# A hybrid decoder step: the norm's gain moved from a GpSimd pass into the weight splits, and gates and scans of two blocks moved to other tiles

## The chip, the cores and the metric

One core of a Trainium2 chip runs the whole program. The metric is the device time of one execution in microseconds (us); lower is better. TensorE (PE) multiplies, VectorE (DVE), ScalarE (ACT) and GpSimd (POOL) do the rest, SyncE (SP) only issues transfers.

## The reference, cut to what matters

```python
def rmsnorm(x, g):
    y = xf * lax.rsqrt(jnp.mean(xf * xf, axis=-1, keepdims=True) + EPS)
    return (y * g.astype(jnp.float32)).astype(x.dtype)

xn = rmsnorm(x, norm_gain)                       # x: 16 meta + 2048 prompt tokens, 8x8 sample tokens, 1024 features
proj = jnp.einsum('btd,dp->btp', xn, w_in)       # 9 groups of 512 columns, and 8 gate columns
yc, conv_new = short_conv(gc * hc, conv_buf, conv_w)
y_conv = gb * yc * jax.nn.silu(zc)
h, state = mlstm_seq(q, k, v, ig, lf, state)     # chunks of 128 tokens, 4 heads of 128, state carried over
y_m = (rms(h) * mh_norm_gain * sigmoid(o)) * silu(zm)
out = jnp.einsum('btw,wd->btd', jnp.concatenate([y_conv, y_m], axis=-1), w_out)
return x + out, ...                              # then a final rmsnorm
```

Since `norm_gain` has one factor for each feature, that is for each row of `w_in`, the kernel multiplies it into the weights and not into the tokens.

## The kernel before, in words

Features lie on the 128 partitions, as KT = 8 groups k of 128 (`w[:, k, :]`). Every float32 operand of the projection is held as a sum of two float16 parts, high and low (`xTh`, `xTl` for the tokens, `Wh`, `Wl` for the weights, the latter scaled by WS = 64), and every product is three matmuls: high-high, low-high, high-low, at L824 to L826 (for the V tile L833 to L835).

The projection is done by **head group** g = 0 to 3 (128 columns of each of nine column groups). A head group has nine **weight tiles**, in the order K, V, Q, GC, HC, GB, ZC, O, ZM (t = 0 to 8), and four **blocks** b of 512 prompt tokens. `pe_block(g, b)` goes over the nine tiles, 24 matmuls of 512 columns each, into one of two PSUM banks in turn (`PB`); it waits on `p_free` until ACT or DVE has emptied the bank of two tiles earlier. In b = 0 each tile also gets a small product for the 80 meta and sample tokens into the bank `T0` ("mix"). Between the halves and at the ends of tiles TensorE does the recurrent part: transposes at L868, the arguments of the exponentials (A), scores (S), and at the ZC and O tiles four `chunk` steps (L887, L888, L893), each of which waits until DVE's `update` has brought the state `cn` forward for the chunk before.

Nothing is scheduled: each engine runs its own written list, in the order of tiles (`at_half`, `evacuate`, `at_end`), joined by semaphores. DVE and ACT wait for their own previous instruction before each one (class `Order`: `did` and `mark` count, `settle` waits; all of them are recorded at L163). So whatever stands first in an engine's list and waits, holds up all that is behind it.

**Weights.** A tile of `w_in` (128 x 1024 float32) is loaded into one of three buffers `wst`. Then three engines work on it in turn: POOL multiplies it by `gain` in place (`gain_w`, L610), ACT writes the high part `Wh` (`split_w`, one activation with scale 64), DVE writes the low part `Wl` = 64 w - Wh (`split_w`, one SCALAR_TENSOR_TENSOR). Only when DVE is done (`w_low`) may the buffer be loaded again. The nine tiles of head group 0 are split at the start and during block 0: t = 0 ahead of the blocks, 1 and 2 too, 3 at the V tile, and 4 to 8 at the half of the tiles Q, GC, HC, GB, ZC (`SPLIT_AT_HALF`). The nine tiles of head groups 1, 2, 3 are split during the last block (b = 3) of the head group before, tile t right after the same tile's own work ("weights blocks" below: (0, 3), (1, 3), (2, 3)); ACT issues the load of tile t + 2 behind its split of tile t.

**Tokens** are normalised in `x_square`, `x_power` (POOL), `x_high_part` (ACT) and `x_low_part` (DVE), and transposed by DMA, one 128-token unit after the other, those of block b + 1 during block b of head group 0.

**Gates.** In blocks 0 to 2 of head group 0, TensorE computes the gate logits of the next block at the end of the tile `GATES_AT[b]` (L849, L850, 16 matmuls into the bank `T1`), ACT and DVE take them from there; DVE runs the cumulative sums and maxima at the tile `SCAN_AT[b]` (`gate_scan`, 7 instructions on 4 partitions) and prepares rows at `TURN_AT[b]` (`gate_turn`, 6 instructions), both ahead of that tile's evacuation. `T1` is used in turn by all these, and in b = 1 also by three rounds of sample states at V, Q, GC (L947), whose results DVE adds to `cs`.

Of the kernel before, what the change touches and what calls it, by code (L numbers as in the profile page):

```python
# [33 lines left out]
ALU = mybir.AluOpType  # L34
ACT = mybir.ActivationFunctionType

P = 128
D = 1024
KT = D // P
# [4 lines left out]
H = 4  # L44
CW = 512
NB, CH = 4, 4
# [4 lines left out]
WS = 64.0  # L51
SK = float(P) ** -0.5
K, V, Q, GC, HC, GB, ZC, O, ZM = range(9)
NT = 9
# [29 lines left out]
GATES_AT = [ZC, HC, HC]  # L84
SCAN_AT = [O, ZC, ZC]
TURN_AT = [ZM, O, O]
# [44 lines left out]
def tok0(b):  # L131
    return MIX + BT * b
# [7 lines left out]
class Order:  # L140
# [11 lines left out]
    def mark(self, instruction, sem, value):  # L152
        self.last = (sem, value)
# [13 lines left out]
def build(nc, x_prompt, x_sample, state_conv, state_c, state_n, state_m, meta, norm_gain, w_in, conv_w,  # L167
# [3 lines left out]
    with ctx:  # L171
        ctx.enter_context(nc.allow_non_contiguous_dma(reason="small parameters and states"))

        def sb(name, shape, dt=F32):
            return ctx.enter_context(nc.sbuf_tensor(name, shape, dt))

        def sem(name):
            return ctx.enter_context(nc.semaphore(name))
# [29 lines left out]

        prow, par = sb("prow", [P, P]), sb("par", [P, STATES_OUT + PARAMS])
# [86 lines left out]
        w_gained, g_gained = sem("w_gained"), sem("g_gained")  # L296
# [284 lines left out]
        def _(pool):  # L581
            made = [0]

            def step(ins):
                ins.then_inc(pool_step, 1)
                made[0] += 1
                pool.wait_ge(pool_step, made[0])
# [18 lines left out]
            def gain_w(g, t):  # L606

                pool.wait_ge(w_in_s[t % STAGES], g * (16 * NT // STAGES) + 16 * (t // STAGES + 1))
                w = wst[t % STAGES]
                pool.tensor_tensor(w[:, :, :], w[:, :, :], gain.unsqueeze(2).broadcast_to([P, KT, P]), ALU.mult).then_inc(w_gained, 1)  # L610

# [5 lines left out]
            gain_w(0, 0)  # L617
# [14 lines left out]
            gain_w(0, 1)  # L632
            gain_w(0, 2)
            step(pool.memset(mparts[:, :], 0.0))
# [21 lines left out]
            gain_w(0, 3)  # L656
            gain_w(0, 4)
            gain_w(0, 5)
            for unit in range(6, 9):
                x_power(unit)  # L660
                gain_w(0, unit)
# [47 lines left out]
            def pool_block(g, b, first, following):  # L709
                def weights(*tiles):  # L710
                    for t in tiles if following == "weights" else ():
                        gain_w(g + 1, t)

                for unit in ((), (11, 12), (15, 16))[b] if first else ():
                    x_power(unit)
                weights(K, V)
# [3 lines left out]
                weights(Q)  # L720
# [6 lines left out]
                weights(GC, HC, GB)  # L727
# [14 lines left out]
                weights(ZC, O)  # L742
# [6 lines left out]
                weights(ZM)  # L749
# [6 lines left out]
            for b in range(NB - 1):  # L756
                pool_block(0, b, True, None)
            for g in range(1, H):
                pool_block(g - 1, NB - 1, False, "weights")
                for b in range(NB - 1):  # L760
                    pool_block(g, b, False, None)
            pool_block(H - 1, NB - 1, False, None)
# [341 lines left out]
        def _(act):  # L1104
# [50 lines left out]
            def split_w(g, t):  # L1155

                act.wait_ge(w_gained, g * NT + (t + 1))
                mark(fn(Wh[:, t, :, :], wst[t % STAGES][:, :, :], ACT.Copy, scale=WS).then_inc(w_high, 1), w_high, g * NT + (t + 1))
# [250 lines left out]
        def _(dve):  # L1409
# [259 lines left out]
            def at_end(g, b, t, first):  # L1669
# [63 lines left out]
                if first:  # L1733
                    if t == GATES_AT[b]:
                        gate_abs(b + 2, BT)
                    if t == ZM and TURN_AT[b] == ZM:
                        gate_turn(b + 2, tok0(b + 1), BT)
                    if t == V:
                        gate_parts(tok0(b))
                    if t == ZM and b == NB - 2:  # L1740
                        gate_parts(tok0(b + 1))
# [76 lines left out]
            dve.wait_ge(t1_full, 1)  # L1818
            mark(copy(par[:, STATES_OUT:], T1[:, 0:PARAMS]).then_inc(t1_free, 1), t1_free, 1)
# [6 lines left out]
            x_low_part(2)  # L1826
            dve.wait_ge(rows_const, 1)
            dve.wait_ge(bias_in, 16 * 3)
            gate_abs(0, MIX)
            x_low_part(3)  # L1830
# [114 lines left out]
```

## Time and profile before

| | us |
|---|---|
| median of 3 runs (lowest, highest) | 1137.95 (1137.59, 1143.83) |
| the profiled execution, its own time | 1141.33 |
| its span in the trace | 1139.5 |
| PE busy | 1071.2 (94%) |
| DVE, ACT, POOL busy | 521.9, 340.3, 325.0 |
| all waits of PE, as the table of waits lists them | 57.2 |

PE is busy nearly all the time, and the other engines less than half of it. A busy share says nothing about when a result is there: the idle time of PE has to be read one gap at a time, with what released it.

### The profile page before, as it was taken

To read this page: it belongs to the slowest core of one execution; us is meant where nothing else is said; L and a number is where in the kernel's file an instruction comes from. 1 tells how busy PE (TensorE), PEld (TensorE's weight loads), DVE (VectorE), ACT (ScalarE), POOL (GpSimd) and SP (SyncE) were. 2 spreads that over 40 slices of the span, in tenths; PEclk is the share of its full clock that TensorE was granted. 3 is DMA by queue.
4 is the path that set the end of the run, shared out by engine and by line. 5 is a ranking of instruction groups with operands and counts; after the bars stand their busy time and mean duration, and the time that the engine had idled before them with its cause. 6 is when DMAs were issued, how large, how long until landed. Compare 5 with 4: busy or idle time off the path is not lost. (4 is left out here: it accounts for less than half of the span.)

```text
span 1139.5 us, 17968 instructions
## 1 busy us (share of the span) xinstructions
PE 1071.2 (94%) x7186; PEld 605.3 (53%) x7186; DVE 521.9 (46%) x981; ACT 340.3 (30%) x672; POOL 325.0 (29%) x370
## 2 busy tenths in 40 slices
PE   2799999998999999879999998899999999999996
PEld 2555546464666555536665655465656565444442
DVE  4886664555453434354433434544333233344333
ACT  6455534242412242322222223332222222221111
POOL 6432403043212323342122223431121111442322
PEclk9899999999999999999999999999999999999998
DMA  9464522043200311442002215310212044255652
GB/s 231 147 138 100 140 71 58 13 121 97 68 20 18 93 43 56 135 115 68 20 18 70 65 56 153 93 32 23 82 47 80 28 140 166 78 191 217 232 208 87
DMA packets 124184, 108.73 MB, mean 95 GB/s; under 512 B 42385, under 2 KB 109093, under 8 KB 124101
## 3 DMA queue, kind: packets, MB, share of 16 engines
q1 hardware_dynamic: 84160, 66.78, 20.1%
q0 software_dynamic: 7600, 25.03, 6.0%
q10 hardware_dynamic: 32340, 15.78, 5.2%
q8 instruction: 57, 0.93, 0.4%
q14 instruction: 27, 0.21, 0.1%
HBM read 65.43 MB, written 33.41 MB: 87 GB/s over the span
## 5 line engine op out<-in xcount | busy, mean ns | idle before, releaser
L824 PE MATMUL bank<-xTh,Wh 128*128 128x512 f16 (+2 forms) x1304 | 423.4, 344 | 7.9 <-DVE u L163 4.1
L825 PE MATMUL bank<-xTl,Wh 128*128 128x512 f16 (+2 forms) x1304 | 425.9, 344 | 0.0
L826 PE MATMUL bank<-xTh,Wl 128*128 128x512 f16 (+2 forms) x1304 | 425.0, 343 | 0.0
L826 PEld LDWEIGHTS bank<-xTh,Wl 128*128 128x128 f16 x1304 | 129.6, 99 | 122.0 <-issue 3.6
L824 PEld LDWEIGHTS bank<-xTh,Wh 128*128 128x128 f16 x1304 | 129.5, 99 | 117.9 <-DVE u L163 5.0
L825 PEld LDWEIGHTS bank<-xTl,Wh 128*128 128x128 f16 x1304 | 129.6, 99 | 109.8 <-issue 4.5
L833 PE MATMUL bank<-Wh,xTh 128*128 128x128 f16 x544 | 92.8, 219 | 1.4 <-DVE ysum L163 1.4
L835 PE MATMUL bank<-Wh,xTl 128*128 128x128 f16 x544 | 92.8, 219 | 0.0
L834 PE MATMUL bank<-Wl,xTh 128*128 128x128 f16 x544 | 92.8, 219 | 0.0
L610 POOL TENSOR_TENSOR wst<-wst,par 128x1024 f32<-128x1024 f32 x36 | 72.1, 2016 | 42.6 <-DMA wst<-in_w_in 42.3
L163 DVE SCALAR_TENSOR_TENSOR Wl<-wst,Wh 128x1024 f16<-128x1024 f32 x36 | 48.1, 1336 | 58.5 <-ACT Wh L163 56.3
L671 POOL DMA_DIRECT2D y_ops<-yst x16 | 11.9, 745 | 184.4 <-DVE yst L163 184.4
L687 POOL TENSOR_TENSOR ysumst<-ysum,ysumst 128x1024 f16<-128x1024 f32 x16 | 34.1, 2130 | 100.5 <-ACT ysumst L163 100.5
L163 ACT ACTIVATE tz<-bank 128x512 f32<-128x512 f32 x32 | 19.1, 598 | 143.1 <-PE bank L826 142.4
L833 PEld LDWEIGHTS bank<-Wh,xTh 128*128 128x128 f16 x544 | 53.2, 98 | 3.5 <-DVE ysum L163 1.9
L834 PEld LDWEIGHTS bank<-Wl,xTh 128*128 128x128 f16 x544 | 53.2, 98 | 1.8
L835 PEld LDWEIGHTS bank<-Wh,xTl 128*128 128x128 f16 x544 | 53.2, 98 | 0.0
L163 ACT ACTIVATE Wh<-wst 128x1024 f16<-128x1024 f32 x36 | 38.0, 1057 | 49.9 <-POOL wst L610 48.0
L163 DVE SCALAR_TENSOR_TENSOR cn<-cn,sel,bank 128x129 f32<-128x129 f32 x64 | 22.4, 350 | 59.9 <-PE bank L893 55.5
L163 DVE SCALAR_TENSOR_TENSOR xs<-bank,xs 128x512 f32<-128x512 f32 x36 | 24.9, 692 | 53.1 <-PE bank L1057 52.7
L669 POOL DMA_DIRECT2D y_ops<-yst x16 | 12.0, 747 | 111.6 <-DVE yst L163 111.6
L748 POOL TENSOR_TENSOR hrs<-hms,halves 128x4 f32<-128x4 f32 x16 | 16.5, 1032 | 88.3 <-DVE hms L163 88.3
(340 smaller groups left out, 1553.3 us busy)
## 6 DMA issues: line engine op xcount, KB each, us to landing
wst<-in_w_in ACTq DMA_DIRECT2D x27, 512.0 KB, 3.8
xs<-in_x_prompt SPq DMA_DIRECT2D x22, 512.0 KB, 4.0
y_ops<-ysumst POOLq DMA_DIRECT2D x16, 512.0 KB, 3.2
w_ops<-xs SPq DMA_DIRECT2D x16, 448.0 KB, 3.8
out<-xs POOLq DMA_DIRECT2D x11, 512.0 KB, 2.9
Wh<-y_ops SPq DMA_DIRECT2D x12, 448.0 KB, 3.6
Wl<-y_ops SPq DMA_DIRECT2D x12, 448.0 KB, 4.3
wst<-in_w_in SPq DMA_DIRECT2D x9, 512.0 KB, 4.9
```

The costliest lines, as they stand in the source:

```text
L163: return op(*operands, **named)
L610: pool.tensor_tensor(w[:, :, :], w[:, :, :], gain.unsqueeze(2).broadcast_to([P, KT, P]), ALU.mult).then_inc(w_gained, 1)
L669: pool.dma_start(ops[:, :, A12 * 2 * P:(A22 + 1) * 2 * P], src).then_inc(out, 16)
L671: pool.dma_start(ops[:, :, 0:2 * P], src[:, :, 0:2 * P]).then_inc(out, 16)
L687: pool.tensor_tensor(parts[:, :, 1, :], ysum[:, :, :, :].rearrange("p r o t -> p (r o) t"), parts[:, :, 0, :], ALU.subtract).then_inc(y_su ...
L748: pool.tensor_tensor(hrs[:, :], hms[:, :], halves[:, :], ALU.pow).then_inc(h_rs, 1)
L824: mm(out, wh[:, k, :], xh, start=(k == 0), stop=False)
L825: mm(out, wh[:, k, :], xl, start=False, stop=False)
L826: last = mm(out, wl[:, k, :], xh, start=False, stop=(k == KT - 1))
L833: mm(out, xh, Wh[:, V, k, :], start=(k == 0), stop=False)
L834: mm(out, xh, Wl[:, V, k, :], start=False, stop=False)
L835: last = mm(out, xl, Wh[:, V, k, :], start=False, stop=(k == KT - 1))
```

## The change

POOL's multiplication (`gain_w`) is gone. `wgain` holds the gain times 64, one column for each k. Since ACT and DVE take one factor for each partition and instruction, a split is now eight instructions of 128 x 128 on ACT, one for each k, and after the eighth has signalled eight on DVE. ACT waits for the transfer itself. Gates, scan and turn of blocks 1 and 2 go to GC, GB and ZC, where they were at HC, ZC and O. Some token parts at the start change places, and the fill of `mparts` has a semaphore of its own.

```diff
-GATES_AT = [ZC, HC, HC]
-SCAN_AT = [O, ZC, ZC]
-TURN_AT = [ZM, O, O]
+GATES_AT = [ZC, GC, GC]
+SCAN_AT = [O, GB, GB]
+TURN_AT = [ZM, ZC, ZC]
...
+        wgain = sb("wgain", [P, KT])
...
-            def gain_w(g, t):
-
-                pool.wait_ge(w_in_s[t % STAGES], g * (16 * NT // STAGES) + 16 * (t // STAGES + 1))
-                w = wst[t % STAGES]
-                pool.tensor_tensor(w[:, :, :], w[:, :, :], gain.unsqueeze(2).broadcast_to([P, KT, P]), ALU.mult).then_inc(w_gained, 1)
...
             def split_w(g, t):
 
-                act.wait_ge(w_gained, g * NT + (t + 1))
-                mark(fn(Wh[:, t, :, :], wst[t % STAGES][:, :, :], ACT.Copy, scale=WS).then_inc(w_high, 1), w_high, g * NT + (t + 1))
+                act.wait_ge(w_in_s[t % STAGES], g * (16 * NT // STAGES) + 16 * (t // STAGES + 1))
+                act.wait_ge(t1_free, 1)
+                for k in range(KT):
+                    last = fn(Wh[:, t, k, :], wst[t % STAGES][:, k, :], ACT.Copy, scale=wgain[:, k:k + 1])
+                    if k < KT - 1:
+                        did(last)
+                mark(last.then_inc(w_high, 1), w_high, g * NT + (t + 1))
...
             split_w(0, 0)
             x_high_part(2)
             x_square(3)
+            x_high_part(3)
+            x_square(4)
             act.wait_ge(bias_in, 16 * 3)
             gate_logits(0, MIX, 1)
-            x_high_part(3)
-            x_square(4)
+            x_high_part(4)
             mixed_start(0, 0, K, True)
-            x_high_part(4)
...
             def split_w(g, t):
 
                 dve.wait_ge(w_high, g * NT + (t + 1))
-                mark(stt(Wl[:, t, :, :], wst[t % STAGES][:, :, :], WS, Wh[:, t, :, :], ALU.mult, ALU.subtract).then_inc(w_low, 1), w_low, g * NT + (t + 1))
+                for k in range(KT):
+                    last = stt(Wl[:, t, k, :], wst[t % STAGES][:, k, :], wgain[:, k:k + 1], Wh[:, t, k, :], ALU.mult, ALU.subtract)
+                    if k < KT - 1:
+                        did(last)
+                mark(last.then_inc(w_low, 1), w_low, g * NT + (t + 1))
```

ACT's list in the weights block (0, 3), from the evacuation of Q to the split of GC (`Wh<-wst` is a split), before:

```order
L163 ACTIVATE qf<-bank 128x512
L163 ACTIVATE dp<-bank,sel 128x128 x4
L163 ACTIVATE eh<-bank,sel 128x128 x4
L163 ACTIVATE Wh<-wst 128x1024
L419 DMA wst<-in_w_in 128x8x128
L163 ACTIVATE ysumst<-ysum 128x8x128
L163 ACTIVATE gcs<-bank 128x512
```

and with the change:

```order
L163 ACTIVATE qf<-bank 128x512
L163 ACTIVATE dp<-bank,sel 128x128 x4
L163 ACTIVATE eh<-bank,sel 128x128 x4
L163 ACTIVATE Wh<-wst,wgain 128x128 x8
L420 DMA wst<-in_w_in 128x8x128
L163 ACTIVATE ysumst<-ysum 128x8x128
L163 ACTIVATE gcs<-bank 128x512
```

The place is the same; one instruction has become eight, and the next load and two evacuations stand behind them.

POOL's list of the same block, with `store_y`, the four sums of `y_operands`, and `store_sums`, before:

```order
L669 DMA y_ops<-yst 128x2x512
L680 TENSOR_TENSOR ysum<-yc,dp 128x2x128
L680 TENSOR_TENSOR ysum<-ysum,yc 128x2x128
L680 TENSOR_TENSOR ysum<-yc 128x2x128
L680 TENSOR_TENSOR ysum<-dp,ysum 128x2x128
L610 TENSOR_TENSOR wst<-wst,par 128x1024
L687 TENSOR_TENSOR ysumst<-ysum,ysumst 128x8x128
L691 DMA y_ops<-ysumst 128x2x1024
L610 TENSOR_TENSOR wst<-wst,par 128x1024 x3
```

and with the change:

```order
L658 DMA y_ops<-yst 128x2x512
L669 TENSOR_TENSOR ysum<-yc,dp 128x2x128
L669 TENSOR_TENSOR ysum<-ysum,yc 128x2x128
L669 TENSOR_TENSOR ysum<-yc 128x2x128
L669 TENSOR_TENSOR ysum<-dp,ysum 128x2x128
L676 TENSOR_TENSOR ysumst<-ysum,ysumst 128x8x128
L680 DMA y_ops<-ysumst 128x2x1024
```

The multiplications are gone, the three of GC, HC and GB among them, which stood behind the sums and their store.

DVE's list in block (0, 1), around the scan (`restart`, `fgain`, `mst`) and the state updates (`cn`), before:

```order
L163 SCALAR_TENSOR_TENSOR cn<-cn,sel,bank 128x129
L163 SCALAR_TENSOR_TENSOR fgain<-gwork,fgain 4x512
L163 SCALAR_TENSOR_TENSOR gcs<-restart,fgain 4x512
L163 COPY fgain<-gwork 4x512
L163 TENSOR_TENSOR fgain<-fgain,gcs 4x512
L163 COPY restart<-gcs 4x3
L163 SCALAR_TENSOR_TENSOR u<-restart,mst,fgain 4x512
L163 TENSOR_TENSOR mst<-gcs,u 4x4
L163 SCALAR_TENSOR_TENSOR ysum<-tz,bank 128x512
L163 SCALAR_TENSOR_TENSOR yc<-yc,ysum 128x512
L163 SCALAR_TENSOR_TENSOR cn<-cn,sel,bank 128x129
```

and with the change, from the end of the scan on:

```order
L163 SCALAR_TENSOR_TENSOR u<-restart,mst,fgain 4x512
L163 TENSOR_TENSOR mst<-gcs,u 4x4
L163 SCALAR_TENSOR_TENSOR yc<-bank,yc 128x512
L163 SCALAR_TENSOR_TENSOR xs<-xs,rsx 128x1024
L163 SCALAR_TENSOR_TENSOR cn<-cn,sel,bank 128x129
L163 COPY arow<-fgain 4x512
L163 TENSOR_TENSOR gwork<-fgain,u 4x512
L163 TENSOR_TENSOR drl<-mst,selh 4x16
L163 SCALAR_TENSOR_TENSOR gwork<-gcs,u 4x512
L163 TENSOR_TENSOR rl<-mst,u 4x4
L163 TENSOR_TENSOR drl<-rl,selh 4x16
L163 SCALAR_TENSOR_TENSOR ysum<-tz,bank 128x512
```

The scan now stands ahead of GB's evacuation and of the first update of `cn`, and between the first update and the second stand the turn's six instructions in place of the scan's seven.

## Rows read from the trace of the kernel before

**Rows 1.** Page: busy time of the engines.

```profile
PE 1071.2 (94%) x7186; PEld 605.3 (53%) x7186; DVE 521.9 (46%) x981; ACT 340.3 (30%) x672; POOL 325.0 (29%) x370
```

**Rows 2.** Groups of instructions: the three passes over the weights (busy, mean ns | idle before).

```profile
L610 POOL TENSOR_TENSOR wst<-wst,par 128x1024 f32<-128x1024 f32 x36 | 72.1, 2016 | 42.6 <-DMA wst<-in_w_in 42.3
L163 ACT ACTIVATE Wh<-wst 128x1024 f16<-128x1024 f32 x36 | 38.0, 1057 | 49.9 <-POOL wst L610 48.0
L163 DVE SCALAR_TENSOR_TENSOR Wl<-wst,Wh 128x1024 f16<-128x1024 f32 x36 | 48.1, 1336 | 58.5 <-ACT Wh L163 56.3
```

**Rows 3.** Groups with a factor for each partition, 128 wide, from SBUF.

```profile
L163 ACT ACTIVATE dp<-dp,sel 128x128 f32<-128x128 f32 x48 | 19.3, 401 | 1.6
L163 DVE SCALAR_TENSOR_TENSOR cs<-cs,dselm,bank 128x129 f32<-128x129 f32 x32 | 11.2, 349 | 5.4 <-PE bank L947 3.8
```

**Rows 4.** Timeline: such instructions in a row (start, length together, count).

```profile
309.63 1.70 ACT L163 ACTIVATE dp<-dp,sel 128x128 f32<-128x128 f32 x4
362.52 1.12 DVE L163 SCALAR_TENSOR_TENSOR cs<-cs,dselm,bank 128x129 f32<-128x129 f32 x3 [1.25 <-PE bank L947]
```

**Rows 5.** Timeline, start and block (0, 0): scan, POOL beside it; PE's waits.

```profile
41.25 6.89 POOL L610 TENSOR_TENSOR wst<-wst,par 128x1024 f32<-128x1024 f32 x3
42.14 1.94 DVE L163 COPY fgain<-gwork 4x512 f32<-4x512 f32 x1
44.12 2.27 DVE L163 TENSOR_TENSOR fgain<-fgain,gcs 4x512 f32<-4x512 f32 x1
46.42 1.75 DVE L163 COPY restart<-gcs 4x3 f32<-4x3 f32 x1
...
52.45 0.55 PE L859 MATMUL bank<-ident,arow 4*128 4x4 f32 x4 [6.58 <-DVE drl L163]
...
80.75 0.45 PE L975 MATMUL bank<-v1m,dpm 80*80 80x129 f32 x2 [0.94 <-DVE dpm L163]
...
114.64 0.23 PE L833 MATMUL bank<-Wh,xTh 128*128 128x128 f16 x1 [1.37 <-DVE ysum L163]
```

**Rows 6.** Timeline of DVE: the same three steps of the next block's scan.

```profile
101.36 0.42 DVE L163 COPY fgain<-gwork 4x512 f32<-4x512 f32 x1
101.81 0.68 DVE L163 TENSOR_TENSOR fgain<-fgain,gcs 4x512 f32<-4x512 f32 x1
102.52 0.16 DVE L163 COPY restart<-gcs 4x3 f32<-4x3 f32 x1
```

**Rows 7.** Timeline, block (0, 1): DVE at GC, and PE's wait at O.

```profile
138.31 0.73 DVE L163 SCALAR_TENSOR_TENSOR cs<-cs,dselm,bank 128x129 f32<-128x129 f32 x2
...
162.51 0.49 PE L887 MATMUL bank<-v,dp 128*128 128x129 f32 x2 [1.67 <-DVE cn L163]
```

**Rows 8.** Timeline of the weights block (0, 3): POOL, ACT, PE's two waits.

```profile
236.42 1.90 POOL L610 TENSOR_TENSOR wst<-wst,par 128x1024 f32<-128x1024 f32 x1 [6.45 <-DMA wst<-in_w_in]
259.67 1.06 ACT L163 ACTIVATE Wh<-wst 128x1024 f16<-128x1024 f32 x1 [4.56 <-POOL wst L610]
271.81 0.49 PE L887 MATMUL bank<-v,dp 128*128 128x129 f32 x2 [0.79 <-DVE cn L163]
281.23 0.49 PE L887 MATMUL bank<-v,dp 128*128 128x129 f32 x2 [2.63 <-DVE cn L163]
```

**Rows 9.** Timeline of PE: the first two of four waits of the weights block (1, 3).

```profile
472.04 0.63 PE L868 MATMUL bank<-ident,kf 128*128 128x128 f32 x4 [2.95 <-DVE dp L163]
494.47 0.61 PE L824 MATMUL bank<-xTh,Wh 128*128 128x512 f16 x1 [2.56 <-DVE u L163]
```

**Rows 10.** Waits of PE, the largest in all (us in total, times, longest).

```profile
PE bank L887 <- DVE cn L163: 14.5, 8, 3.1
PE bank L868 <- DVE dp L163: 6.6, 2, 3.7
...
PE bank L824 <- DVE u L163: 4.1, 2, 2.6
```

**Rows 11.** Sums of the stretch of block (1, 3): PE, PEld, DVE, ACT, POOL busy; clock.

```profile
462.00:520.00 58.00, 49.23 (x277) 26.09 (x275) 24.71 (x35) 19.27 (x33) 25.99 (x18) 0.91 0.45 122
```

More of the change, by code:

```diff
@@ L295, in build @@
         xt_in = [sem(f"xt_in{i}") for i in range(3)]
-        w_gained, g_gained = sem("w_gained"), sem("g_gained")
+        g_gained, parts_clear = sem("g_gained"), sem("parts_clear")
         w_in_s = [sem(f"w_in{i}") for i in range(STAGES)]
@@ L616, in _ @@
             pool.tensor_tensor(wgst[:, :, :], wgst[:, :, :], gain.unsqueeze(2).broadcast_to([P, KT, 2 * H]), ALU.mult).then_inc(g_gained, 1)
-            gain_w(0, 0)
             x_power(2)
@@ L631, in _ @@
             x_power(4)
-            gain_w(0, 1)
-            gain_w(0, 2)
-            step(pool.memset(mparts[:, :], 0.0))
+            pool.memset(mparts[:, :], 0.0).then_inc(parts_clear, 1)
+            pool.wait_ge(parts_clear, 1)
             step(pool.memset(maskb[:, :], 0.0))
@@ L655, in _ @@
             x_power(5)
-            gain_w(0, 3)
-            gain_w(0, 4)
-            gain_w(0, 5)
             for unit in range(6, 9):
                 x_power(unit)
-                gain_w(0, unit)
             def store_y(g, b, part):
@@ L707, in store_mixed, with pool_block @@
                 pool.dma_start(dst, ystm[:, part, :, :]).then_inc(out, 16)
[L709 to L712, printed above, removed]
+            def pool_block(g, b, first):
                 for unit in ((), (11, 12), (15, 16))[b] if first else ():
                     x_power(unit)
-                weights(K, V)
                 if not (first and b == 0):
@@ L719, in pool_block @@
                     y_operands(g if b else g - 1, b - 1 if b else NB - 1)
-                weights(Q)
                 for unit in ((), (13,), ())[b] if first else ():
@@ L726, in pool_block @@
                     x_power(unit)
-                weights(GC, HC, GB)
                 if b == 0:
@@ L741, in pool_block @@
                 store_y(g, b, 0)
-                weights(ZC, O)
                 if (g, b) in SLAB_FIRST:
@@ L748, in pool_block @@
                 pool.tensor_tensor(hrs[:, :], hms[:, :], halves[:, :], ALU.pow).then_inc(h_rs, 1)
-                weights(ZM)
                 if b == 0:
@@ L756, in _ @@
             for b in range(NB - 1):
-                pool_block(0, b, True, None)
+                pool_block(0, b, True)
             for g in range(1, H):
-                pool_block(g - 1, NB - 1, False, "weights")
+                pool_block(g - 1, NB - 1, False)
                 for b in range(NB - 1):
-                    pool_block(g, b, False, None)
-            pool_block(H - 1, NB - 1, False, None)
+                    pool_block(g, b, False)
+            pool_block(H - 1, NB - 1, False)
             store_y(H - 1, NB - 1, 1)
@@ L1738, in at_end @@
                     if t == V:
+                        if b == 0:
+                            dve.wait_ge(parts_clear, 1)
                         gate_parts(tok0(b))
@@ L1818, in _ @@
             dve.wait_ge(t1_full, 1)
+            did(ts(wgain[:, :], T1[:, 0:KT], WS, None, ALU.mult))
             mark(copy(par[:, STATES_OUT:], T1[:, 0:PARAMS]).then_inc(t1_free, 1), t1_free, 1)
@@ L1826, in _ @@
             x_low_part(2)
+            x_low_part(3)
             dve.wait_ge(rows_const, 1)
@@ L1829, in _ @@
             gate_abs(0, MIX)
-            x_low_part(3)
             x_low_part(4)
```

## The prediction

> **What bounds the kernel now.** I read the page's busy times first [rows 1]: TensorE is busy 1071 of 1139.5 us, so nothing else can be the bound in the mean, and only its gaps can move the time. The span stands 1.8 us below that execution's own time, 1141.3; the median is 1137.95. I work out differences and add them to the median. Next the waits of PE, in the timeline. They add up to 57 us: 17 at the very start, for parameters and the first transposed tokens, then a dozen gaps of 1 to 7 us, each ended by a late DVE result. The reader is to see where: one of 6.6 us behind the first scan, 0.9 and 1.4 around block (0, 0) [rows 5], 1.7 at the same place in (0, 1) [rows 7] and (0, 2), and 22 us in the three weights blocks: the table of waits has 14.5 for the state `cn`, 6.6 before L868, 4.1 for `u` [rows 10], and 14.5 less those two of 1.7 makes 11.2 + 6.6 + 4.1 = 21.9. Of it 0.8 + 2.6 = 3.4 are in (0, 3) [rows 8], 2.95 + 2.56 [rows 9] + 0.2 + 3.1 = 8.8 in (1, 3), and so 9.7 in (2, 3). Last, what DVE waits for there: for ACT's high part, 56 us in all, ACT for POOL's product 48, POOL for the load 42 [rows 2]. So the three passes over a tile are a chain through three lists, and what stands behind a split waits with it.
>
> **The price of a split.** Removed: 36 passes of POOL at 2.02 us, 72 us [rows 2]. None is on PE's path by itself; it counts as the first link of the chain. Added: no row shows such a piece, but its neighbours are close. Four ACT instructions of 128 x 128 from SBUF with a per-partition operand take 1.70 us, one takes 0.40 [rows 3, 4]: one starts every (1.70 - 0.40)/3 = 0.43. Eight: 7 x 0.43 + 0.40 = 3.44 against 1.06, so +2.4. On DVE three of 128 x 129 take 1.12, one 0.35: one each 0.385, eight 3.05 against 1.23 to 1.34, so +1.8. The bounds of a split: not below the one long instruction (1.06, 1.23), if the pieces overlapped wholly; not above eight with a gap of 0.1 each (4.0, 3.6). I take 3.44 and 3.05, since those rows have the same width, memory and wait on the step before. The chain of a tile is then 3.44 + 3.05 = 6.5 where it was 2.02 + 1.06 + 1.34 = 4.4, and a tile of PE lasts 5.2 (24 matmuls at 0.215). ACT gets 36 x 2.4 = 86 us more work, DVE 62.
>
> The Trainium skill, "VectorE: DVE Perf Modes", in its section on the errata for SBUF sources, says that each instruction from SBUF pays a fixed latency, so that many small tiles pay it many times, and its table would give a ScalarE piece (224 + 128)/1.2 = 293 ns, eight 2.35 us. The row has 401 ns; by the page the (0, 3) sum below would be about nothing rather than +6.
>
> **The weights blocks.** ACT has in (1, 3) 19.3 us of work and DVE 24.7 in 58 [rows 11]; with nine splits 19.3 + 21.4 = 41 and 24.7 + 16.4 = 41. There is room, but not in the order of the lists. I walk through (0, 3), each step being the later of its inputs plus its length, 0.1 between instructions. K: weights land at 236.4 [rows 8]; ACT 237.4 to 240.8, DVE to 243.9. V: product with `G` to 244.7, ACT's copies to 246.1, pieces to 249.6, DVE to 252.7. Q: ACT evacuates to 250.3, eight exponentials to 253.7, pieces to 257.2; DVE to 260.3. GC: `ysumst` and `gcs` to 259.1, pieces to 262.7; DVE 265.8. Before, ACT stood idle here 4.6 us for POOL and began at 259.67 [rows 8], so this is where POOL's absence pays, and still ACT ends 2 us later. HC: DVE empties the bank at 266.8; PE is ready for ZC at 265.0: **wait 1.85**. Conv to 269.3, pieces to 272.4; GB: pieces to 276.3, then only the first update of `cn`, 276.8; PE was there at 272.7: **4.1** (before 0.8). ZC's split ends on ACT at 282.6, DVE 285.7, third update 286.1, PE there at 283.3: **2.8** (before 2.6). The last bank is emptied 0.7 late for the next V. Sum 9.5 against 3.4: **+6**.
>
> In (1, 3) weights land later in the block, when PE is in the V tile. DVE's product with `G` stands behind the K split, which without POOL's link starts 2.0 earlier, but takes 2.4 + 1.8 more: 2.3 later. So the wait before L868 grows from 2.95 [rows 9] to 5.3. The exponentials wait for the mask, which waits for the split of V, so ACT is free for GC's bank only when PE needs it: 3.7, new. Then 2.5, 4.1, 2.8 and 0.7 as above: 19.2. The same walk with before's lengths gives 10.0 where the trace has 8.8, so I count the difference of the walks, **+9.2**, and the same for (2, 3): **+9.2**.
>
> **Start and block (0, 0).** The low part of unit 2 comes behind the first split, +0.5 for PE. DVE's splits of V and Q, 1.8 longer each, stand ahead of the first scan; in the scan three steps took 1.94, 2.27, 1.75 beside POOL's product [rows 5], and take 0.42, 0.68, 0.16 without it [rows 6]: -4.7. So the rows are ready 1.5 earlier, 50.7; but the split of t = 3 and the factors come behind, and at the end of Q only -0.3 is left. From there ACT works without a pause, 53.8 to 68.5 (split 3.44, token parts 2.4, `qf`, eight exponentials 3.2, small ones, split 3.44). DVE waits for it, then works without a pause through two splits, two token parts, the conv (15.6 us, with 14 gaps 16.9) to `dpm` at 85.4. PE has been waiting since 81.2 and goes on at 85.5, where it went on at 80.75 [rows 5]: +4.7. The next split delays the meta tokens' state by 1.4 and the first update by 0.6; then ACT's and DVE's last split stand before the gates of the next block, whose scan starts at 108.9, and the bank of ZM is free for the next V at 124.1, before at 114.64 [rows 5]. Sum **+9.5** (+6.7 if the scan catches up).
>
> **The moved gates.** The chain at ZC was update, scan (4.7 us), evacuation, update: the wait of 1.7 [rows 7]. In (0, 2), where no sample states and token parts stand between, the scan is over at GB, the turn is 2.5: no wait, **-1.7**. In (0, 1) the gates now need `T1` right behind the sample states, whose sums DVE has only at 139.04 [rows 7], 1.3 after PE could begin: +1.3. The scan, behind a token part, ends at 155.5, GB and another token part follow, and the first update comes 0.6 late, the second 1.35 late: together 3.25 for 1.67, **+1.6**. The table is worth nothing in the sum.
>
> **Sum.** 9.5 + 1.6 - 1.7 + 6 + 9.2 + 9.2 = +34: 1137.95 + 34 = **1172**. Not in it: the clock. In (1, 3) it is 0.91 in the mean [rows 11], that is 10 us of 58 at the lower of its two levels, 1.2 instead of 2.4 GHz, behind waits of 2.6 and 3.1; it costs up to 5 us. I count 8 more waits of over 2.5; at 1.7 each for two in three, +9 is the upper bound, part of which DVE's lateness would cover.
>
> **Rivals.** *POOL was the bound (faster, 1124).* DVE's steps beside POOL's products are stretched, and the chain's first link goes. The Trainium skill, "SBUF — State Buffer", section "Who interferes with whom", has the port shared by the two as an exclusive lock; the trace agrees with rows 5 and 6. For it: ACT's 48 us for POOL [rows 2]. Price: a walk with splits of 2.2 and 2.0 us gives -2 in (0, 3), -4 in the others; with the start -1.5 and a table at -1.7, -13. It decides below about 0.28 us for a piece; rows 4 show 0.43. *The room takes it up (same, 1145).* With 2.9 and 2.6 for a split the walk gives +0.4 and twice +3, block (0, 0) some +2, table 0: +7. Against: again rows 4. *Everything is late and the clock falls too (1181):* +34 and +9.
>
> **How the numbers follow.** Forecast 0.64, with the clock 0.15, same 0.12, faster 0.09. A measurement tells 1% (11.4 us) from no change. Slower by over 1%: 0.79. The range leaves out the faster case and half of the same one: low 1147; at the top it takes in the clock and the upper bound of the pieces in part (4.0 and 3.6 throughout would be 1200): 1190.
>
> **What would show it.** In the changed profile: `Wh<-wst,wgain` x288 near 400 ns and `Wl` x288 near 350; POOL some 72 us less; DVE about 580; PE's waits near 90 us, those for `cn` at the end of the ZC tile of each weights block about 4, one before L868 of 5; PE at L975 near 85; no wait in (0, 2) at the third chunk. Wrong if pieces start closer together than 0.3 us, or if GpSimd had been the late one in places where I take DVE to be.

## The result, and the profile after

The changed kernel takes **1170.68 us** (median of 4 runs, 1169.04 to 1171.18), the kernel before, on the same chip, 1139.63 (4 runs, 1137.59 to 1143.83): ratio 1.0265, 95% interval 1.0231 to 1.0299. The profiled execution has a span of 1169.5 us where before it was 1139.5: +30.0; the medians of this chip differ by 31, with +34 forecast.

Busy times and the two groups of the splits, from the page of the changed kernel (they answer to [rows 1] and [rows 2]):

```profile
PE 1081.2 (92%) x7186; PEld 608.4 (52%) x7186; DVE 560.2 (48%) x1234; ACT 417.8 (36%) x924; POOL 246.8 (21%) x334
L163 ACT ACTIVATE Wh<-wst,wgain 128x128 f16<-128x128 f32 x288 | 115.6, 401 | 18.5 <-DMA wst<-in_w_in 4.5
L163 DVE SCALAR_TENSOR_TENSOR Wl<-wst,wgain,Wh 128x128 f16<-128x128 f32 x288 | 107.9, 375 | 77.2 <-ACT Wh L163 65.9
```

POOL lost 78 us. ACT no longer waits for it (48.0 in [rows 2]) and gained 77.5 us of work. DVE gained 38: 60 for longer splits, while its other steps are 21 us shorter, among them those that lay beside POOL's products [rows 5, 6]. What it waits for ACT's high part grew from 56 to 66 us. PE's work is the same 7186 matmuls, yet it is busy 10 us longer: its granted clock is at the lower level for some 20 us more than before.

The largest waits of PE in the changed kernel (us in total, times, longest), to be held against [rows 10]:

```profile
PE bank L867 <- DVE cn L163: 12.9, 8, 4.0
...
PE bank L848 <- DVE dp L163: 11.4, 2, 6.5
PE bank L804 <- DVE u L163: 7.6, 3, 2.7
...
PE bank L804 <- ACT gcs L163: 4.9, 2, 2.6
PE bank L955 <- DVE dpm L163: 3.9, 1, 3.9
PE bank L839 <- DVE drl L163: 3.7, 1, 3.7
...
PE bank L813 <- ACT kfm L163: 2.4, 3, 0.8
```

With the small ones they add up to 77 us, against 57 before: +20, and +10 of PE's own time makes the +30. The waits for the state `cn` are even smaller, and the one behind the first scan fell from 6.6 [rows 5] to 3.7; new are the ones for `gcs` and `kfm`, both copies by ACT, and the one at L955 (4 us where [rows 5] have 0.94).

Where it came in: sums over stretches that run from PE's first transposes of `eh` in one block to those of another, so both tables cut the program at the same instructions. Kernel before, then the changed one: start and (0, 0); (0, 3); (1, 3); (2, 3); the last turn. Columns: stretch, length, busy time (and instructions) of PE, PEld, DVE, ACT, POOL, granted clock, DMA share, GB/s.

```profile
0.00:117.30 117.30, 87.05 (x779) 57.04 (x780) 80.65 (x148) 64.92 (x108) 46.69 (x77) 0.96 0.62 150
...
239.20:297.20 58.00, 54.58 (x382) 31.31 (x380) 31.75 (x48) 20.51 (x37) 25.84 (x18) 1.00 0.31 86
463.20:531.20 68.00, 59.23 (x382) 32.64 (x380) 32.10 (x49) 22.03 (x38) 27.33 (x19) 0.92 0.41 114
697.10:764.40 67.30, 57.64 (x382) 32.39 (x380) 32.82 (x49) 22.03 (x38) 26.86 (x19) 0.95 0.38 111
764.40:1139.50 375.10, 363.95 (x2167) 191.82 (x2164) 136.72 (x261) 73.70 (x158) 93.67 (x110) 0.99 0.34 120
```

```profile
0.00:125.70 125.70, 90.82 (x780) 59.15 (x781) 85.15 (x212) 84.30 (x171) 23.10 (x68) 0.93 0.57 140
...
247.80:312.40 64.60, 57.44 (x381) 32.17 (x380) 42.33 (x105) 38.99 (x96) 8.96 (x10) 0.95 0.27 73
478.40:552.60 74.20, 59.84 (x380) 32.59 (x378) 42.73 (x106) 41.41 (x101) 8.95 (x10) 0.93 0.34 93
718.60:794.30 75.70, 60.18 (x380) 32.51 (x378) 43.00 (x106) 41.40 (x101) 8.95 (x10) 0.91 0.34 98
794.30:1169.50 375.20, 363.98 (x2168) 191.80 (x2164) 138.18 (x268) 73.69 (x158) 93.62 (x110) 0.99 0.35 120
```

The loss sits where weights are split: +8.4, +6.6, +6.2, +8.4. Blocks (0, 1) and (0, 2) in between, where the table acts, come to +0.2 together, and the last turn, without splits, is the same to 0.1 us. In every one of the three weights blocks ACT goes from 21 to 40 us and DVE from 32 to 43 in 65 to 75: far from full, and still late. PE's busy column says how much of a stretch is clock: 2.9 of the 6.6 in (0, 3), 3.8 of the 8.4 at the start, 0.6 of the 6.2 in (1, 3) and 2.5 of the 8.4 in (2, 3).

PE's six waits of block (1, 3) in the changed kernel's timeline (start, length, instruction, idle time before it and what ended it), which answer to [rows 9]:

```profile
489.22 1.09 PE L848 MATMUL bank<-ident,kf 128*128 128x128 f32 x4 [4.95 <-DVE dp L163]
508.10 0.39 PE L804 MATMUL bank<-xTh,Wh 128*128 128x512 f16 x1 [2.59 <-ACT gcs L163]
516.15 0.42 PE L804 MATMUL bank<-xTh,Wh 128*128 128x512 f16 x1 [2.70 <-DVE u L163]
526.21 0.49 PE L867 MATMUL bank<-v,dp 128*128 128x129 f32 x2 [2.35 <-DVE cn L163]
535.64 0.49 PE L867 MATMUL bank<-v,dp 128*128 128x129 f32 x2 [0.97 <-DVE cn L163]
548.60 0.22 PE L813 MATMUL bank<-Wh,xTh 128*128 128x128 f16 x1 [0.80 <-ACT kfm L163]
```

And two splits of (0, 3), ACT's and DVE's, in the timelines of the two engines; the second DVE row is the split that lies beside GpSimd's `store_sums` (L676, a difference over 128 x 1024):

```profile
254.81 3.44 ACT L163 ACTIVATE Wh<-wst,wgain 128x128 f16<-128x128 f32 x8
258.28 3.60 DVE L163 SCALAR_TENSOR_TENSOR Wl<-wst,wgain,Wh 128x128 f16<-128x128 f32 x8 [3.49 <-ACT Wh L163]
265.99 4.81 DVE L163 SCALAR_TENSOR_TENSOR Wl<-wst,wgain,Wh 128x128 f16<-128x128 f32 x8 [2.52 <-ACT Wh L163]
267.26 2.22 POOL L676 TENSOR_TENSOR ysumst<-ysum,ysumst 128x1024 f16<-128x1024 f32 x1 [8.25 <-ACT ysumst L163]
```

### The profile page after: what moved, and what is told of

Its sections match the earlier page's. It is cut to its first block and busy times, and to the rows that moved or that the text cites. A ratio compares the mean times of both kernels' runs of the same rounds, so it can differ in the third digit from the quotient of the medians.

```text
span 1169.5 us, 18465 instructions
## 1 busy us (share of the span) xinstructions
PE 1081.2 (92%) x7186; PEld 608.4 (52%) x7186; DVE 560.2 (48%) x1234; ACT 417.8 (36%) x924; POOL 246.8 (21%) x334
## 5 line engine op out<-in xcount | busy, mean ns | idle before, releaser
L163 DVE SCALAR_TENSOR_TENSOR Wl<-wst,wgain,Wh 128x128 f16<-128x128 f32 x288 | 107.9, 375 | 77.2 <-ACT Wh L163 65.9
L163 ACT ACTIVATE Wh<-wst,wgain 128x128 f16<-128x128 f32 x288 | 115.6, 401 | 18.5 <-DMA wst<-in_w_in 4.5
L163 ACT ACTIVATE tz<-bank 128x512 f32<-128x512 f32 x32 | 19.1, 598 | 146.6 <-PE bank L806 145.6
L676 POOL TENSOR_TENSOR ysumst<-ysum,ysumst 128x1024 f16<-128x1024 f32 x16 | 34.4, 2147 | 117.4 <-ACT ysumst L163 117.4
L867 PE MATMUL bank<-v,dp 128*128 128x129 f32 x128 | 25.9, 284 | 12.9 <-DVE cn L163 12.9
```

Source lines behind the costliest of these rows:

```text
L163: return op(*operands, **named)
L676: pool.tensor_tensor(parts[:, :, 1, :], ysum[:, :, :, :].rearrange("p r o t -> p (r o) t"), parts[:, :, 0, :], ALU.subtract).then_inc(y_su ...
L867: mm(out, dp[:, c * P:(c + 1) * P], v1[:, c, :], start=True, stop=False)
```

## The experiments

My theory was that the length of the two splits is the whole loss, through two channels: in the weights blocks a tile's chain ACT to DVE (6.5 us) is longer than PE's 5.2 us a tile, a threshold; in block (0, 0) the two engines work without a pause and every added us counts. Rivals: the loss of GpSimd as first link and the moved table; the added work as such; the clock. All ratios are against runs of the kernel before on the same chip, whose median moved between 1138.7 and 1142.4 us; differences of medians below are made from the ratios, at 1140 us. The table at the end gives all twelve.

**Both splits short, no factors.** In `split_w` of the changed kernel:

```
-                for k in range(KT): ... Wh[:, t, k, :] ... scale=wgain[:, k:k + 1]
+                mark(fn(Wh[:, t, :, :], wst[t % STAGES][:, :, :], ACT.Copy, scale=WS).then_inc(w_high, 1), ...)
-                for k in range(KT): ... Wl[:, t, k, :] ... wgain[:, k:k + 1] ...
+                mark(stt(Wl[:, t, :, :], wst[t % STAGES][:, :, :], WS, Wh[:, t, :, :], ...).then_inc(w_low, 1), ...)
```

> The changed kernel, but both splits are one long instruction again, scaled by the constant: the norm's feature factors are left out of the weights altogether (they stay in the gates' weights). GpSimd has no product either, and the order of everything else is that of the change. My theory (the length of the two splits is the whole loss): the walk through the lists with splits of 1.06 and 1.25 us gives no wait at all but 1.1 before L848, so blocks (0, 3), (1, 3), (2, 3) stand 3.5, 8.9 and 8.9 below the kernel before; with the start and block (0, 0) 1 to 4 below it, some 22 to 25 us under the kernel before: 1115 to 1118. If the loss comes from the order or from GpSimd's absence, it stays above 1150. If GpSimd's products had cost nothing at all before, it comes out at 1139.

1108.79 us, ratio 0.9733 (0.9713 to 0.9754). That is 6 us below my range: -3.9, -13.3 and -9.2 in the three weights blocks (forecast -3.5, -8.9, -8.9), -6.1 up to the end of block (0, 0) (forecast -1 to -4). The length of the splits is the loss, and more than the loss: the changed kernel (1.0265) stands 61 us above this run, its own skeleton, and the kernel before 30. GpSimd's products had a price of their own, which the change did remove.

**Only one of the two in pieces.**

> The changed kernel, but VectorE's low part is one instruction scaled by the constant; the feature factors are left out of the low part alone. ScalarE's eight pieces stay. My theory: a tile's chain is 3.44 + 1.25 = 4.7 us, under PE's 5.2, so nearly all of the loss goes although ScalarE has all of its added work: the walk gives -1.7 and twice -1.8 against the kernel before in the weights blocks, with block (0, 0) between -1 and +4: 1133 to 1140. A rival in which ScalarE's work alone is the loss and VectorE only follows gives 1160 or more.

> The mirror of the last: ScalarE's high part is one instruction with the constant (the feature factors are left out of the high part), VectorE's eight pieces stay. Chain of a tile 1.06 + 3.05 = 4.1. My theory: the walk gives -2.3 and twice -2.5 against the kernel before; block (0, 0) between -1 and +4, since there DVE had the gapless stretch: 1132 to 1140. With the last run it says whether the two lengths add (each would then bring half of the loss, 1155) or only their sum over a tile of PE counts.

1134.40 (0.9963, 0.9950 to 0.9976) and 1143.83 (1.0046, 1.0029 to 1.0063). From the skeleton, pieces on ACT cost 26 us, pieces on DVE 36, both together 61. In the weights blocks against the kernel before they gave -1.0, -4.6, -3.5 and -0.9, -1.8, +0.9, where both together give +6.6, +6.3, +8.4: neither alone brings the three blocks above where they were before, in sum -9.1 and -1.8 against +21.3. The second came out 4 us above my range, and the surplus is in the weights blocks (-1.8 where I had -7.3; the 3.6 at the start lie inside my -1 to +4). In each of the three, two of DVE's nine splits lie beside GpSimd's work and take 4.8 us instead of 3.06, and the mean piece is 388 ns.

The two runs also say something against my threshold. Their chains, 4.7 and 4.1 us, are both under PE's 5.2, and yet each costs its part: the weights blocks stand 17 and 25 us above the skeleton's, and 26 + 36 = 62 us is what both together cost (61). The added lengths add up; nothing in these runs begins at 5.2 us.

**The table.** The changed kernel with the old table, and the kernel before with the new one:

```
-GATES_AT = [ZC, GC, GC]      SCAN_AT = [O, GB, GB]      TURN_AT = [ZM, ZC, ZC]
+GATES_AT = [ZC, HC, HC]      SCAN_AT = [O, ZC, ZC]      TURN_AT = [ZM, O, O]
```

> The changed kernel with the gates, scans and turns at the tiles of the kernel before. My theory: (0, 1) gets 1.6 to 2.1 us back and (0, 2) loses 1.7 to 1.9: within 1 us of the changed kernel, 1170 to 1171. If longer splits and the table act together (a scan at GB stands between splits), it is 3 to 6 us off in either direction.

> The kernel before with the changed table and nothing else of the change. In the changed kernel the table gave one block 2.2 us and took them from another. With the short splits of the kernel before: the wait of 1.65 before the third update goes in (0, 2), and (0, 1) has 1.0 to 3.2 for 1.7: between -1.7 and +1.5, not to be told from the kernel before.

1171.17 (1.0286, 1.0270 to 1.0301) and 1141.85 (1.0003, 0.9989 to 1.0018). The table moves 2 us from one block to its neighbour: (0, 1) is +2.1 with it and 0.0 without, (0, 2) -1.9 with it and +0.3 without. Its worth cannot be told from nothing.

**The chain shortened, the work left.**

```
                 for k in range(KT):
-                    ... did(last)                                  # ScalarE: one signal behind the eighth
+                    mark(last.then_inc(w_high, 1), w_high, (g * NT + t) * KT + (k + 1))
...
-                dve.wait_ge(w_high, g * NT + (t + 1))              # VectorE: ahead of the loop
+                    dve.wait_ge(w_high, (g * NT + t) * KT + (k + 1))
```

> The changed kernel, full computation, with one thing new: each of ScalarE's eight pieces raises the semaphore by itself, and VectorE waits for each piece instead of for the eighth. All work of both engines stays as it is (ACT 3.44, DVE 3.05 a tile), only the chain of a tile falls from 3.44 + 3.06 = 6.5 to about 3.44 + 0.4 = 3.9 us where VectorE is free. My theory (the chain against PE's 5.2 us a tile): nearly the whole loss goes, 1134 to 1146. Rival: the room on the two engines is what lacks, that is 86 + 62 us of added work; then little changes, 1160 to 1170.

1156.18 (1.0121, 1.0106 to 1.0136): neither range. In the weights blocks +2.7, +1.0, +2.5 are left of +6.6, +6.3, +8.4: there the shorter chain gave back 15 of 21 us. At the start +9.5 instead of +8.4, nothing regained. PE's wait before L955 stays (timeline of PE in this run, then its DVE group):

```profile
84.39 0.45 PE L955 MATMUL bank<-v1m,dpm 80*80 80x129 f32 x2 [4.28 <-DVE dpm L163]
```

```profile
L163 DVE SCALAR_TENSOR_TENSOR Wl<-wst,wgain,Wh 128x128 f16<-128x128 f32 x288 | 108.2, 376 | 52.1 <-ACT Wh L163 22.4 <-DVE Wl L163 1.0
```

The edit did not leave DVE's work as it was, though, as its timeline shows:

```profile
39.81 3.55 DVE L163 SCALAR_TENSOR_TENSOR Wl<-wst,wgain,Wh 128x128 f16<-128x128 f32 x8
```

A piece now waits for ACT's semaphore and for its own predecessor, and one starts every 0.455 us where it was 0.387, also in this split, whose eight high parts had all been ready for 6.7 us. A split of DVE is 3.54 us instead of 3.06; the nine of head group 0 take 4.8 us longer in all. So this run understates what the chain is worth, and by itself it does not show that at the start only the work counts. The pair of runs without own waits, below, is the clean one.

**The own waits.** In the changed kernel each piece raises its engine's step semaphore and the next piece waits for it. Taken out on both engines:

```
                     last = fn(Wh[:, t, k, :], ...)
-                    if k < KT - 1:
-                        did(last)
```

> The changed kernel, full computation, without the waits of a piece on the piece before it on the same engine (they write different parts of a tile). It tells what the fixed cost of a piece is. If it is that wait, ACT's pitch falls from 0.43 to well under 0.3 and DVE's from 0.385 as well, splits of 2.2 and 2.0, and the kernel comes near 1140. If a piece's own fixed time is inside its 401 ns and does not overlap with the next, only the gap of 0.03 to 0.04 goes: 3.2 and 2.8 to 2.9 a split, 1163 to 1168. I hold the second more likely.

1134.39 (0.9928, 0.9913 to 0.9943), 38 us under the changed kernel. I had held the other outcome more likely, so this is the miss that taught most. Groups and one split of each engine in this run:

```profile
L163 ACT ACTIVATE Wh<-wst,wgain 128x128 f16<-128x128 f32 x288 | 88.0, 388 | 15.7 <-DMA wst<-in_w_in 8.0 <-PE bank L806 3.7 <-ACT Wh L163 0.5
L163 DVE SCALAR_TENSOR_TENSOR Wl<-wst,wgain,Wh 128x128 f16<-128x128 f32 x288 | 87.5, 375 | 50.0 <-ACT Wh L163 47.7 <-DVE ycm L163 0.5
```

```profile
266.70 2.44 ACT L163 ACTIVATE Wh<-wst,wgain 128x128 f16<-128x128 f32 x8 [2.73 <-PE bank L806]
...
266.98 2.19 DVE L163 SCALAR_TENSOR_TENSOR Wl<-wst,wgain,Wh 128x128 f16<-128x128 f32 x8
```

The mean of a piece has hardly changed (401 to 388, 375 to 375), but 288 x 388 ns would be 112 us and the group's busy time is 88: the pieces now overlap. A new one starts every (2.44 - 0.39) / 7 = 0.293 us on ACT instead of 0.434, every (2.19 - 0.35) / 7 = 0.263 on DVE instead of 0.386.

**Both of the last two.** Pieces signalled one by one, and no own waits:

> Full computation: the changed kernel without the waits of a piece on its predecessor and with ScalarE's pieces signalled one by one. A split then is 2.45 us on ACT and VectorE follows 0.4 behind where it is free. My theory (threshold of a tile's chain against PE's 5.2, and in block (0, 0) the work of the engines itself): the run without own waits left 13 us of PE's waits in the weights blocks; a shorter chain takes most of them: the walk with 2.44 + 0.4 gives -3.5 and twice -8 against the kernel before, the start +0.3: 1118 to 1128. If the waits for each piece cost as much as the own waits did, a split of VectorE is back at 3 us and it stays at 1130 to 1140.

1120.37 (0.9812, 0.9788 to 0.9836): inside the range, with the full computation 52 us under the changed kernel and 21 under the one before. The chain's gain, 16 us in `piece_by_piece`, is there a second time, 13 us, and here DVE's splits stay 2.19 us. By block it is 10.0 in the three weights blocks and 0.9 up to the end of block (0, 0). There PE's waits are 3.3 us shorter, but its clock is at the lower level for 7 us more, so the chain's worth at the start, 1 to 3 us, is small beside the 8 us that the shorter splits alone gave there (+8.4 to +0.3). The run also says which half of the own wait costs. ACT's pieces each raise a semaphore here and still start every 0.292 us, so raising it is free, and waiting for the predecessor is what cost 0.14; DVE's pieces each wait for ACT's semaphore, and where ACT is ahead they still start every 0.263. (PE's waits left in the weights blocks of `no_self_waits` add up to 15.8 us in its trace, not the 13 of my expectation; here 9.3 are left.)

**Where the 30 us of the kernel before were.** GpSimd's products kept, but into a tile that nobody reads:

```
-                pool.tensor_tensor(w[:, :, :], w[:, :, :], gain..., ALU.mult).then_inc(w_gained, 1)
+                pool.tensor_tensor(spare, w[:, :, :], gain..., ALU.mult).then_inc(w_gained, 1)
...
-                act.wait_ge(w_gained, g * NT + (t + 1))
+                act.wait_ge(w_in_s[t % STAGES], ...)
```

> The kernel before, but GpSimd writes its 36 products to a tile that nobody reads, and ScalarE waits for the load instead (only the reload of the raw tile waits for the product). The weights go without the feature factors; GpSimd's work and its traffic stay. The two tiles of the gates' chain that lay in that memory lie in free partitions elsewhere, and the last gain vector is loaded later. It divides the 30 us between the kernel before and the run without factors: if they were the wait for the product as a link of the chain, 1109 to 1116; if they were VectorE's steps stretched beside the products, 1130 to 1139. I expect 1113 to 1120: the start and block (0, 0) keep some 5 us of stretched steps.

1123.56 (0.9839, 0.9822 to 0.9855), 4 above what I expected. So 18 us were the link. The other 12, up to `no_gain`, are mainly the products' presence beside VectorE, but not proved to be it alone: in this run a reload still waits for the product, and the token parts at the start stand as before the change. DVE's group of splits in this run, and in the one without products:

```profile
L163 DVE SCALAR_TENSOR_TENSOR Wl<-wst,Wh 128x1024 f16<-128x1024 f32 x36 | 53.7, 1493 | 30.0 <-ACT Wh L163 27.7
```

```profile
L163 DVE SCALAR_TENSOR_TENSOR Wl<-wst,Wh 128x1024 f16<-128x1024 f32 x36 | 46.1, 1280 | 34.5 <-ACT Wh L163 32.7
```

That is 8 us of DVE's time in splits, nearly all in the weights blocks. Some 4 us of the twelve are at the start (-1.7 here, -6.1 without products), where the first scan is stretched beside the products [rows 5, 6].

**The factors elsewhere.** Three ways of keeping the computation with short splits:

> Full computation. The factors enter the tokens instead of the weights: GpSimd multiplies each raw unit of tokens (17 of them, all in the first turn) by the factors' row before ScalarE's high part, both splits of the weights are single instructions, and the gates' weights take no factors either. The table is that of the change. From the run without factors (1109): the products stand before the first tokens' high part, some 2 us a unit, so the start gives up 2 to 6 us and the first turn 0 to 4: 1111 to 1119. If GpSimd's 17 products hold up the first turn as its 36 did before, 1125 or more.

> ScalarE's high part is one instruction with the constant (no factors in it), VectorE's low part is eight pieces without own waits, the factors stand in the low part, which then holds the whole rest. Chain 1.06 + 2.2 to 2.4. The walk gives -2.9 and twice -6.1 against the kernel before, block (0, 0) and the start -1 to +2: 1122 to 1128. If VectorE's pieces are what costs in any case (with own waits the same kernel took 1144), 1135 or more.

> ScalarE as in the last. VectorE makes its low part in two instructions over the whole tile: the product of the raw tile with the factors, broadcast, into a spare tile, which needs only the load and so lies beside ScalarE's copy, then the difference to the high part. 2 x 1.15 to 1.25 = 2.3 to 2.5 us on VectorE, of which 1.2 waits for nobody: the chain of a tile is 1.1 + 1.2. As the last or a little below: 1118 to 1126. If the product waits for loads at the head of VectorE's list and holds up what stands behind, 1130 or more.

`x_product` took 1133.96 (0.9921, 0.9904 to 0.9938), 15 above my range; the other two 1122.75 (0.9838, 0.9817 to 0.9859) and 1120.00 (0.9813, 0.9793 to 0.9834), as forecast. `dve_early` also qualifies what the section on the change says: one factor for each partition and instruction holds for the scaling operand; as a second, broadcast tensor VectorE takes all eight factors of a row in one instruction over the tile. With the factors in the tokens the weights blocks lose nearly all their waits (0.45 us is left in (1, 3), 2.65 in (2, 3)), and block (0, 3) has none; as a stretch,

```profile
258.30:312.40 54.10, 54.10 (x383) 31.50 (x381) 26.83 (x48) 20.25 (x36) 9.73 (x10) 1.00 0.34 99
```

but up to the end of block (0, 1) the run is 20 us longer than before. GpSimd waits first for the row of factors, then each product is 2.35 us, some up to 3.2, ahead of the tokens that PE waits for; in its timelines of POOL and PE:

```profile
8.05 0.18 POOL L604 TENSOR_SCALAR msx<-ssx 80x1 f32<-80x1 f32 x1 [5.19 <-DMA fgain<-in_norm_gain]
8.86 2.33 POOL L608 TENSOR_TENSOR xs<-xs,fgain 80x1024 f32<-80x1024 f32 x1
...
67.93 3.22 POOL L608 TENSOR_TENSOR xs<-xs,fgain 128x1024 f32<-128x1024 f32 x1
```

```profile
32.62 0.26 PE L805 MATMUL bank<-xTh,Wh 128*128 128x128 f16 x1 [4.64 <-DMA xTl<-to]
38.48 0.38 PE L830 MATMUL bank<-xTh,Wg 128*128 128x512 f16 x1 [2.98 <-DMA xTl<-yst]
```

In `dve_pieces`, `low_no_waits` and `dve_early` the high part holds no factors and the low part takes all the rest, so it is a larger number than in either kernel given, and the product of two low parts, which this kernel leaves out, weighs more; by how much was not measured. `both` has no such change.

**All runs by block**, each against the kernel before, us of span from the profiled executions, cut at PE's first transposes of `eh`; the medians come from different chips, and the ratios given above compare them:

| run | start, (0, 0) | (0, 1) | (0, 2) | (0, 3) | (1, 3) | (2, 3) | sum | median |
|---|---|---|---|---|---|---|---|---|
| changed | +8.4 | +2.1 | -1.9 | +6.6 | +6.3 | +8.4 | +29.9 | 1170.7 |
| old_table | +8.2 | 0.0 | +0.3 | +6.6 | +6.5 | +8.0 | +29.6 | 1171.2 |
| piece_by_piece | +9.5 | +0.5 | -1.9 | +2.7 | +1.0 | +2.5 | +14.3 | 1156.2 |
| dve_pieces | +3.6 | +2.1 | -1.9 | -0.9 | -1.8 | +0.9 | +2.0 | 1143.8 |
| table_alone | -0.7 | +2.1 | -1.9 | +1.7 | -3.6 | +0.4 | -2.0 | 1141.9 |
| act_pieces | +1.8 | +3.0 | -1.9 | -1.0 | -4.6 | -3.5 | -6.2 | 1134.4 |
| no_self_waits | +0.3 | +3.1 | -1.9 | -2.0 | -4.2 | -1.8 | -6.5 | 1134.4 |
| x_product | +11.5 | +8.6 | -1.0 | -4.0 | -13.6 | -9.0 | -7.5 | 1134.0 |
| scratch | -1.7 | 0.0 | +0.1 | -2.0 | -7.8 | -6.9 | -18.3 | 1123.6 |
| low_no_waits | -2.2 | +2.1 | -1.9 | -3.4 | -7.8 | -4.7 | -17.9 | 1122.8 |
| both | -0.6 | +3.1 | -2.0 | -3.7 | -9.3 | -5.0 | -17.5 | 1120.4 |
| dve_early | +1.2 | +2.1 | -1.9 | -3.4 | -8.8 | -8.9 | -19.7 | 1120.0 |
| no_gain | -6.1 | +3.0 | -1.9 | -3.9 | -13.3 | -9.2 | -31.4 | 1108.8 |

`table_alone` shows the noise of single cells: nothing in it touches the weights blocks, and they differ by up to 3.6 us, since waits and clock fall differently in each execution. All rows are differences to one execution of the kernel before, whose block (1, 3) has 8.8 us of waits and 10 us at the lower clock, where `table_alone` has 6.5 and 7: some 3 us of each value in that column may be this. Sums and medians carry the argument.

## Why the prediction was right, point by point

- *The price of a split, 3.44 and 3.05.* Measured 3.44 and 3.06 where nothing is beside. The pitch of the neighbours' rows [rows 3, 4] was the right thing to take, because those pieces also wait for their predecessor. (The VectorE row is not wholly from SBUF, as its heading and the forecast have it: one of its inputs is a PSUM bank. Its pitch, 0.385, was the same as the measured 0.387 all the same.) Missed was DVE's split beside GpSimd's work for the sums: 3.3 to 4.8. Without the own waits, a case the forecast did not consider, the same pieces take 2.44 and 2.19.
- *Start and block (0, 0), +9.5.* Measured +8.4, with PE going on behind the first scan at 50.39 (forecast 50.7), at L955 at 84.55 (forecast 85.5, 80.75 before) and at the next V at 123.00 (forecast 124.1). But 3.8 of the 8.4 are slower work of PE, where the forecast had waits alone.
- *The moved gates, +1.6 and -1.7.* Measured +2.1 and -1.9, by the mechanism given: in (0, 1) the gates wait 1.27 for the sample states, in (0, 2) PE has no wait. Both table runs show it.
- *Weights blocks, +6, +9.2, +9.2.* Measured +6.6, +6.3, +8.4. The places were right (before L848, at the start of GB and ZC, at the updates, at the next block), the waits too large: in (1, 3) 4.95, 2.59, 2.70, 2.35, 0.97, 0.80, sum 14.4, against 5.3, 3.7, 2.5, 4.1, 2.8, 0.7, which is 19.1 and not the 19.2 written. The last but one wait of (0, 3) was 0.16 where I had 2.8.
- *Room on the two engines.* The stretch of [rows 11], 462 to 520, holds seven of DVE's nine splits and is not the whole block, which is 68 us long with 32.1 us of DVE and 22.0 of ACT. With my added lengths DVE comes to 48.5 of it and not 41. It was 42.7, since its other steps became shorter; for the same reason DVE is busy 560 us in all and not 580. That there is room stays true.
- *The clock, left out of the sum.* PE's busy time rose by 10 us; the forecast had +9 as an upper bound on top of +34. It is the term that failed in kind: it came, but in the place of waits. The reading that fits the trace is that DVE catches up while PE works at half clock behind one wait, and the next wait is shorter: the third update's wait, 2.8 in my walk, was 0.16 behind 6.8 us at the lower clock in (0, 3), and 0.97 and 0.95 behind 3.4 us of it in (1, 3) and (2, 3). No run tested it by itself. The forecast of 90 us of waits became 77 and 10 of slower work. The two errors, waits too large by 14 (34 more forecast, 20 measured) and the clock at nothing where it took 10, nearly cancel. The forecast worked out no such exchange, so that 1172 lies as near as 1 us to 1170.7 is luck; the places, the direction and the size of the loss are not.
- *Rivals "the room takes it up" and "everything late and clock too".* The first would have needed splits of 2.9 and 2.6, which the changed kernel does not have; its terms (+0.4, twice +3, +2) add up to +8.4 and not +7, so 1146. The second had the clock on top of all waits; it came in their place.
- *A misreading.* Not each of PE's gaps before was ended by a late DVE result: two in the first 27 us, 1.4 and 2.5, ended with a transfer of tokens. With the change they are 1.0 and 2.6, so nothing in the sum hangs on it.
- *Rival "GpSimd was the bound".* I gave it a small chance and a price of -13 for splits of 2.2 and 2.0 us, and said that none of its passes is on PE's path by itself. The side of the forecast is right, but GpSimd's part was sized too small: without the link and the products 30 us go (`no_gain`), where my walk with the short splits had 22 to 25, and 18 of them are the link. The change did gain that, and lost 61 to the pieces. Its condition, pieces below 0.28 us apart, was a little too strict: at 0.293 and 0.263 the kernel is already 0.7% faster than before.

## What to carry to other kernels

An operation that is spread over two engines in series can hold up its consumer when its chain gets longer, whatever the engines' busy shares say. Here that began well below the consumer's time for a tile, because other steps that the consumer needs stand behind the operation in the engines' lists. Where the engines have no pause, their work counts, and the shorter chain gave back 1 to 3 us of its 13. Before cutting an instruction into pieces, take the pitch of such pieces from the trace, and ask what part of it is a wait that the pieces do not need: independent pieces want one signal behind the last for the same engine, and a signal each for the next one. Check in the trace that a run that was to change one thing left the rest alone: `piece_by_piece` was meant to shorten a chain and made one engine's pieces slower. Moving work to a free engine can be right and still lose to what is added elsewhere; a run that leaves the work out altogether says how much there was to win.

## What the runs showed of the hardware

- A wait of a piece on its predecessor on the same engine cost 0.14 us on ScalarE (start to start 0.434 with, 0.293 without) and 0.12 on VectorE (0.386 and 0.263), at 128 x 128 elements. The Trainium skill, "VectorE: DVE Perf Modes", section "The DRAIN you can't avoid", has it that leaving out the semaphores between chained VectorE operations saves nothing, measured there on eight copies. Here it saves 0.87 us of 3.06, so the measurement decides for pieces of this size and form.
- With both waits on each piece, the one on its predecessor and one on ScalarE's semaphore, VectorE's pieces started every 0.455 us (`piece_by_piece`), with the first alone every 0.387 (changed kernel), and with the second alone every 0.263 where ScalarE was ahead (`both`).
- For ScalarE the trace agrees with the Trainium skill, "ScalarE: Activation LUTs", section "What ACT_TABLE_LOAD costs": 186 ns + 0.833 ns an element, 93 ns more for a per-partition operand and 93 ns of overlap back to back give, as an estimate, 386 ns a piece and 293 ns from start to start; the rows have 388 and 293. The 293 ns that the prediction took from the other page as the length of a piece are no piece's length here; they equal its pitch without a wait.
- A split of VectorE beside one instruction of GpSimd over 128 x 1024 took 4.81 us instead of 3.06, and all of the difference lies in one of its eight pieces; the one-instruction split had a mean of 1493 ns beside 36 products of GpSimd and of 1280 without them.
- The granted clock was 1.00 in block (0, 3) before and 0.95 after, with the two waits of 2.2 and 4.0 us in it; in the whole changed run but its end, each fall to the lower level began in or within 1.1 us behind a wait of PE of 2.3 us or more. This is no rule: the wait of 2.59 us in (1, 3) had no fall behind it, and in `no_self_waits` one fall began at 126.9 behind a wait of 1.2 us that ended at 125.45. Whether a kernel would be faster if it kept the clock up was not tried.
